# First stage in pieces as its loads land, and the output norms of two of three mixers moved out of the stage behind the third

## The chip, the cores and the metric

The kernel runs on one core of one Trainium2 chip. The metric is the time of one execution on the device in microseconds (us), the median of three runs. Smaller is better. Engines are called PE (TensorE: matmuls; PEld is its weight load), DVE (VectorE), ACT (ScalarE), POOL (GpSimd) and SP (SyncE, which here only starts DMAs).

## The reference

One inference step of a network of two layers over 640 tokens: 128 context tokens and 512 latent ones, model width 1024, float32. In a layer, `_ada` gives shift, scale and gate from a conditioning vector; the three mixers work on column groups of one projection; each ends in a group norm and a gate.

```python
def _rms_norm(x, g, eps=1e-6):
    xf = x.astype(jnp.float32)
    y = xf * lax.rsqrt(jnp.mean(xf * xf, axis=-1, keepdims=True) + eps)
    return (y * g.astype(jnp.float32)).astype(x.dtype)

def _group_norm(y, g, n_groups, center, eps=1e-5):
    yf = y.reshape(y.shape[:-1] + (n_groups, y.shape[-1] // n_groups))
    if center: yf = yf - jnp.mean(yf, axis=-1, keepdims=True)
    yf = yf * lax.rsqrt(jnp.mean(yf * yf, axis=-1, keepdims=True) + eps)
    return yf.reshape(y.shape) * g

mod = silu(cond) @ ada_w + ada_b                       # six vectors of 1024: sh1, sc1, g1, sh2, sc2, g2
h = _rms_norm(x, norm1_g) * (1 + sc1) + sh1
u = h @ w_in                                           # 1024 x 3296
# SSD (Mamba-2), 8 heads of 64, 512 columns, forward and backward scan over chunks of 128 tokens
y_ssd = _group_norm((y_f + y_b + d_skip * xs) * silu(z), ssd_norm_g, 2, center=False)
# RWKV-7, 4 heads of 64, 256 columns
y_rwkv = _group_norm(o_f + o_b, rwkv_norm_g, 4, center=True) * gate
# mLSTM, 4 heads of 64, 256 columns
y_ml = _group_norm(h_f + h_b, mlstm_norm_g, 4, center=True) * sigmoid(o)
x = x + g1 * (concat([y_ssd, y_rwkv, y_ml]) @ w_out)
h = _rms_norm(x, norm2_g) * (1 + sc2) + sh2
x = x + g2 * ((silu(h @ ffn_w1) * (h @ ffn_w3)) @ ffn_w2)
```

Outputs are the normed `x` of both token groups and the final states of the context scans of each layer and direction.

## The kernel before

All engines are programmed by hand. Each has one stream of instructions, and they wait on semaphores; nothing is reordered by a planner, so the order is the written one.

**Layout.** `x` stays in SBUF feature-major: 8 tiles (KT) of 128 features by 640 tokens. Tokens go in five chunks of 128 (NC), chunk 0 being the context. `U` holds the projected tiles: Z to Z+3 the SSD's gate, XS to XS+3 its values, later its output, MV and MV+1 mLSTM's output, BT_ and CT_ RWKV's, and LORA, MISC, MO the gates. `arena` is one area that is used again and again.

**Weights.** SP loads blocks of 128 columns (512 KB) in the order of the list BLOCKS into a ring of four slots (`ring`); ada_w's groups g (512 columns, four units each) have slots of their own. A product in full precision is three fp32r matmuls: ScalarE's `split` (line 1647) writes the high part of a weight block to `whi`, GpSimd (line 810) the low part in place, and TensorE does high·high, high·low, low·high (`mm3`, lines 928 to 930) over two halves of 320 tokens. The activations have high and low parts too (`rwp_r`, `arena_r`; for w_out `rp_r` and `U_r`).

**Stages of a layer,** times of the first in us:
- 0 to 57, in the first layer alone: loads, 40 transposes of `x` (line 826), squares (ScalarE, 1603), sums over features by VectorE (2001) and by ones products (`norm_sum`, 848 and 852), root (1608), reciprocal, the row spread to all partitions (`norm_rows`, 879), the product with `x` (1989); ada_w's groups 0, 2, 1, 3 (`ada_unit` 892, `ada_pick` 900, `ada_copy` 1634); ScalarE writes h (`norm_out`, 1622). GpSimd builds the constants first (553 to 642) and counts them in `setup["pool"]`, which others wait on up to POOL_SET.
- to about 290: the projections, 26 blocks in the order of ORDER. The first is the mixed block MISC (RWKV's last 64 columns, dt, mLSTM's gates), whose pieces SP loads as runs of 16 to 256 bytes, in six transfers.
- to 395: the scans of SSD and mLSTM chunk by chunk. TensorE makes scores, VectorE multiplies by weights (2273), then SSD's product of 16 (line 1183) and mLSTM's; `normalise` (2314 is its last instruction) divides mLSTM's output by its denominator, and four products by `ident` (1240) add both directions and turn the result to feature-major.
- to 580: RWKV in five rounds of 37 us, one for each chunk. In each, products of keys and masks (VectorE 2384 to 2395, 2412, 2425), an inversion by repeated products (TensorE 1317, VectorE's additions 2405), then the output, added to U (2458).
- 580 to 613: the norms of all three mixers' outputs. The mean of BT_/CT_ and MV/MV+1 by block sums (`g_job`, TensorE 1462, float32), the centring (VectorE 2475), squares, sums, root of 640 columns (ScalarE, 1892 on), reciprocal (2488), the spreading (1462), the scaling of eight tiles with gains (2505) and gates (2510), the low parts (2493). GpSimd's `gates` multiplies SSD's four tiles by Z beforehand.
- w_out (8 blocks; the third block's split comes only when a block before it is done), the second norm, the FFN (to about 1150).

The lines that say how the first stage begins:

```python
pe.wait_ge(setup["in"], 80)                  # all of x and three small loads
...
pe.wait_ge(setup["par"], 16 * DEPTH * (len(PROWS) + 2))   # parameters of both layers
...
norm_sum(0)
norm_rows(0)
pe.wait_ge(setup["pool"], POOL_SET)
pe.wait_ge(setup["dve"], 1)
for i, g in enumerate(EARLY):
    for u in range(UNITS):
        ada_unit(0, g, u)
```

Of the kernel before, what the change touches and what calls it, by code (L numbers as in the profile page):

```python
# [22 lines left out]
F32 = mybir.dt.float32  # L23
F32R = mybir.dt.float32r
BF16 = mybir.dt.bfloat16
ALU = mybir.AluOpType
# [3 lines left out]
P = 128  # L30
# [46 lines left out]
for _name, _rows in (("ada_b", 48), ("norm1_g", 8), ("norm2_g", 8), ("ssd_conv_w", 18), ("ssd_conv_b", 6),  # L77
# [18 lines left out]

POOL_IDENT, POOL_SET = DEPTH + 3, 87
# [3 lines left out]
    "g_mm": 14, "g_read": 6, "g_rec": 2, "g_sq": 8, "g_src": 1, "g_std": 2, "gated": 1, "inv_add": 50,  # L101
# [9 lines left out]
    "y_done": 8, "y_half": 4, "y_hi": 8, "y_lo": 8, "y_mm": 5, "ym_ready": 5, "yr_mm": 10, "yr_read": 10,  # L111
    "ys_read": 5, "yt_mm": 5, "yt_read": 5,
# [7 lines left out]
    "pair_mm", "pair_read", "tmp_act", "tmp_dve", "feat_ready", "k_scaled",  # L120
    "rows_act", "rows_dve", "kk_sq", "lora_x", "rw_ready",
# [6 lines left out]
    "g_src", "g_sq", "g_mm", "g_read", "g_std", "g_done", "wo_mm", "wo_read", "ffn_mm", "ffn_silu", "ffn_ready",  # L128
# [4 lines left out]
def build(nc, io):  # L133

    with ExitStack() as ctx:
        def sb(name, n):
# [6 lines left out]
                 ("pool", "in", "par", "cs", "mm", "read", "dve", "act")}  # L143
# [4 lines left out]
                  for l in range(DEPTH)]  # L148

# [22 lines left out]
        NSD, NRC = sb("NSD", NC), sb("NRC", NC)  # L172
        SELr = ctx.enter_context(nc.sbuf_tensor("SEL", [P, 6 * NC], F32R))
# [69 lines left out]
        YM = ar(8960, 512).rearrange("p (d n) -> p d n", d=2)  # L243

# [35 lines left out]
        SQUARES = [gtmp[:, 0, :], gtmp[:, 1, :], U[:, Z + 2, :], U[:, Z + 3, :]]  # L280
# [24 lines left out]
        EARLY = [0, 2, 1, 3]  # L305
        UNITS = KT // 2
# [9 lines left out]
        BLOCKS = [(0, "ada_w", g, u) for g in EARLY[:2] for u in range(UNITS)]  # L316
        BLOCKS += [(0, "w_in", m) for m in ORDER[:2]]
# [25 lines left out]
        for n, b in enumerate(BLOCKS):  # L343
# [15 lines left out]
            total[q] += 16 * (6 if b[1:] == ("w_in", MISC) else 1)  # L359
# [13 lines left out]
        at_block = {b: n for n, b in enumerate(BLOCKS)}  # L373
        SPLIT = [n for n, b in enumerate(BLOCKS) if b[1] != "ada_w"]
# [8 lines left out]
        POST = [m for m in ORDER if m in CONV or m in SHIFT]  # L383
        YTILES = [XS, XS + 1, XS + 2, XS + 3, BT_, CT_, MV, MV + 1]
        SHIFTED = {m: i for i, m in enumerate(SHIFT)}
# [8 lines left out]
        with nc.Block() as block:  # L394
            @block.sync
            def _(sp):
# [3 lines left out]
                def state(name, l):  # L400
# [3 lines left out]
                sp.dma_start(xi[:, 0, :], io["x_prompt"].rearrange("a t f -> (a t) f")).then_inc(setup["in"], 16)  # L404
                sp.dma_start(xi[:, 1:NC, :], io["x_sample"].rearrange("a (c p) f -> p (a c) f", p=P)).then_inc(
                    setup["in"], 16)
# [6 lines left out]
                for lay in range(DEPTH):  # L413
# [52 lines left out]

                    def rwkv_out():
# [23 lines left out]
                    for n in range(first_, end_):  # L491
                        blk = BLOCKS[n]
                        l, name = blk[0], blk[1]
                        if blk == (0, "w_in", ORDER[2]):
                            sp.wait_ge(setup["pool"], POOL_SET)
                            small_loads(0)
                        if blk == (lay, "w_in", ORDER[24]):
                            rows_out()
                        if blk == (lay, "w_out", 0):
                            rows_in()  # L500
                            states_in()
                            states_out()

                            sp.wait_ge(s["yt_read"], at["yt_read"] + NC)
                        if blk == (lay, "w_out", RING):
                            rwkv_out()
# [17 lines left out]
                        if blk[1:] == ("w_in", MISC):  # L524
                            gt = C_GATE
                            for at_, n_, src in ((0, 64, C_RW + 896), (64, 16, C_DT)):
                                load(dst[:, :, at_:at_ + n_], w[:, :, src:src + n_], sem)
                            for at_, src in ((80, gt + 4), (112, gt)):
                                load(dst[:, :, at_:at_ + 4], w[:, :, src:src + 4], sem)
                                load(dst[:, :, at_ + 4:at_ + 8], w[:, :, src + 8:src + 12], sem)  # L530
# [17 lines left out]
            def _(pool):  # L548
# [67 lines left out]

                for c, (lo, hi) in enumerate(((0, 8), (8, 16), (16, 20), (20, 24), (0, 16), (16, 24))):
# [28 lines left out]
                for lay in range(DEPTH):  # L646
# [26 lines left out]
                    def gates():  # L673

                        pool.wait_ge(s["yt_read"], at["yt_read"] + NC)
                        pool.wait_ge(s["ys_read"], at["ys_read"] + NC)
                        g.tensor_tensor(U[:, XS:XS + 4, :], U[:, XS:XS + 4, :], U[:, Z:Z + 4, :], ALU.mult).then_inc(
                            s["gated"], 1)
                        pool.wait_ge(s["gated"], at["gated"] + 1)
                        pool.wait_ge(s["rw_ready"], at["rw_ready"] + 1)  # L680
# [9 lines left out]
                    def end_values(c):  # L690
# [8 lines left out]
                        ins.then_inc(s["ve_ready"], 1)  # L699

# [16 lines left out]
                    def scans():  # L717
# [18 lines left out]
                        for c in range(2, NC):  # L736
                            scaled_values(c)
                            skip(c)

# [42 lines left out]

                    n = at_block[lay, "w_in", MISC]
                    if before[n] is not None:
                        sem, value = used[before[n]]
                        pool.wait_ge(sem, value)
                    w = slot(n)
                    g.memset(w[:, :, 88:112], 0.0)
                    g.memset(w[:, :, 120:128], 0.0).then_inc(s["gaps"], 1)
                    for q in range(Q_LAYER):  # L790
# [16 lines left out]
                        q_ = lay * Q_LAYER + q  # L807
# [1787 lines left out]
```

## Time and profile before

| | |
|---|---|
| three runs | 2306.55, 2297.8, 2301.24 us |
| median | 2301.24 us |
| the profiled execution | 2307.51 us, span 2305.8 us |
| mean granted clock of PE | 0.962 of full speed |
| PE busy | 2129.9 us (92%) |
| DVE busy | 836.0 us (36%) |
| ACT busy | 774.3 us (34%) |
| POOL busy | 735.9 us (32%) |

The span is the time between the first and the last record of the profile, and the execution takes a little more. A share is busy time over the whole span, so it says nothing of a single stage; for those, the rows below give stretches.

### The profile page before, as it was taken

Reading aid. Unit: us, or ns where it says so; the run is one execution under the profiler, and the core shown is the slowest. Engines: PE = TensorE matmul, PEld = TensorE weight load, DVE = VectorE, ACT = ScalarE, POOL = GpSimd, SP = SyncE. Lnnn points to the kernel's source line nnn. Section 1 sums busy time; section 2 is a strip of 40 time slices with the busy share of each in tenths; the row PEclk is TensorE's granted clock in tenths of the full one; section 3 lists DMA queues with packets and bytes.
Section 4 is the critical chain, followed back from the end, with each engine's and each line's share of the span. In section 5 each row is a group of like instructions: output and inputs, shape, how many; then the busy total and the mean of one; then the engine's idle time right before and its main releaser. Section 6 shows DMA issues by size and latency. Waiting matters only on the chain.

```text
span 2305.8 us, 46139 instructions
## 1 busy us (share of the span) xinstructions
PE 2129.9 (92%) x20590; PEld 1974.0 (86%) x20590; DVE 836.0 (36%) x1385; ACT 774.3 (34%) x1368; POOL 735.9 (32%) x539
## 2 busy tenths in 40 slices
PE   4999999888789999999979989988888899999999
PEld 4999766778589999999979987667867899999998
DVE  4755265554641111011148443555455311110112
ACT  3535553323333222121144364433332422222212
POOL 4333161324123333333313322522242233333331
PEclk7999998999899999999989999899998899999999
DMA  7454201000012222234335431010001122222222
GB/s 250 147 156 128 63 8 37 6 2 3 19 55 65 80 76 74 74 110 142 104 87 174 148 114 30 1 38 5 3 2 46 50 79 74 74 74 74 73 76 71
DMA packets 260497, 166.67 MB, mean 72 GB/s; under 512 B 29938, under 2 KB 234228, under 8 KB 260300
## 3 DMA queue, kind: packets, MB, share of 16 engines
q1 hardware_dynamic: 259846, 163.59, 23.9%
q8 instruction: 162, 2.65, 0.5%
q14 instruction: 35, 0.29, 0.1%
q10 hardware_dynamic: 454, 0.14, 0.0%
HBM read 159.59 MB, written 4.12 MB: 71 GB/s over the span
## 4 chain that ended last, share of the span: by engine, by line
PE 84%; DVE 7%; ACT 5%; issue 2%; POOL 1%; DMA 0%; another core or an unknown queue 0%; SPq 0%; DVEq 0%; ACTq 0%
PE PS L928 21%; PE PS L929 20%; PE PS L930 20%; PE PS L1317 5%; PE PS L892 2%; PE PS L1462 1%; PE PS L1146 1%; PE PS L1383 1%; PE PS L1335 1%; PE PS L1183 1%; PE PS L989 1%; DVE U L2330 1%; PE PS L1197 1%; POOL ring_r L810 1%; PE PS L1150 1%
## 5 line engine op out<-in xcount | busy, mean ns | idle before, releaser
L928 PE MATMUL PS<-rwp_r,whi_r 128*128 128x320 f32 x2880 | 904.5, 314 | 40.4 <-POOL ring_r L810 16.5
L930 PE MATMUL PS<-rwp_r,ring_r 128*128 128x320 f32 x2880 | 896.6, 311 | 0.0
L810 POOL TENSOR_TENSOR ring_r<-ring,whi_r 128x1024 fp32r<-128x1024 f32 (+1 forms) x204 | 498.5, 2445 | 1139.7 <-ACT whi_r L1647 1139.7
L929 PE MATMUL PS<-arena_r,whi_r 128*128 128x320 f32 x2240 | 697.4, 311 | 0.0
L928 PEld LDWEIGHTS PS<-rwp_r,whi_r 128*128 128x128 f32 x2880 | 547.0, 190 | 56.0 <-issue 28.6
L930 PEld LDWEIGHTS PS<-rwp_r,ring_r 128*128 128x128 f32 x2880 | 546.9, 190 | 0.0
L929 PEld LDWEIGHTS PS<-arena_r,whi_r 128*128 128x128 f32 x2240 | 425.4, 190 | 0.0
L1647 ACT ACTIVATE whi_r<-ring 128x1024 fp32r<-128x1024 f32 (+1 forms) x204 | 211.4, 1039 | 542.1 <-PE PS L930 542.0
L929 PE MATMUL PS<-U_r,whi_r 128*128 128x320 f32 x960 | 298.2, 311 | 0.0
L2542 DVE TENSOR_TENSOR U<-arena,PS 128x640 f32<-128x640 f32 x44 | 36.2, 822 | 549.7 <-PE PS L930 549.7
L929 PEld LDWEIGHTS PS<-U_r,whi_r 128*128 128x128 f32 x960 | 181.8, 189 | 0.0
L1317 PE MATMUL PS<-arena 64*64 64x64 f32 x3840 | 137.2, 223 | 37.3 <-DVE arena L2393 17.1
L1317 PEld LDWEIGHTS PS<-arena 64*64 64x64 f32 x3840 | 124.5, 138 | 50.0 <-DVE arena L2393 19.9
L2001 DVE TENSOR_TENSOR arena<-arena 128x640 f32<-128x640 f32 x30 | 63.1, 2104 | 213.4 <-ACT arena L1603 212.9
L1918 ACT ACTIVATE arena<-PS 128x640 f32<-128x640 f32 x44 | 31.0, 705 | 263.4 <-PE PS L930 263.4
L1676 ACT ACTIVATE U<-PS 128x640 f32<-128x640 f32 x56 | 39.3, 702 | 181.8 <-PE PS L930 181.5
L1849 ACT ACTIVATE arena<-PS 128x512 f32<-128x512 f32 (+1 forms) x100 | 55.5, 555 | 132.7 <-PE PS L1317 132.7
L1817 ACT ACTIVATE arena<-PS,arena 128x128 f32<-128x128 f32 x240 | 65.6, 390 | 77.2 <-PE PS L1150 77.0
L769 POOL TENSOR_TENSOR arena<-arena,MKC 128x256 f32<-128x256 f32 x40 | 36.6, 935 | 145.7 <-DVE arena L2388 145.7
L2521 DVE SCALAR_TENSOR_TENSOR x<-PS,MOD,x 128x128 f32<-128x128 f32 (+2 forms) x96 | 36.0, 431 | 125.2 <-PE PS L930 125.2
L2065 DVE SCALAR_TENSOR_TENSOR arena<-U,PC,arena 128x127 f32<-128x127 f32 x80 | 61.9, 794 | 24.8 <-ACT arena L1688 22.9
L2405 DVE TENSOR_TENSOR arena<-arena,PS 128x256 f32<-128x256 f32 x100 | 40.4, 419 | 69.8 <-PE PS L1317 69.8
(383 smaller groups left out, 2667.7 us busy)
## 6 DMA issues: line engine op xcount, KB each, us to landing
ring<-in_ffn_w SPq DMA_DIRECT2D x120, 512.0 KB, 3.8
rwp<-in_ada_w SPq DMA_DIRECT2D x64, 512.0 KB, 4.8
ring<-in_w_in SPq DMA_DIRECT2D x50, 512.0 KB, 4.4
U<-in_ada_w SPq DMA_DIRECT2D x16, 512.0 KB, 9.7
ring<-in_w_out SPq DMA_DIRECT2D x16, 512.0 KB, 4.6
arena<-in_ada_w SPq DMA_DIRECT2D x16, 512.0 KB, 4.7
ring<-in_ffn_w SPq DMA_DIRECT2D x16, 384.0 KB, 3.3
out<-arena SPq DMA_DIRECT2D x5, 512.0 KB, 2.6
```

The costliest lines, as they stand in the source:

```text
L810: g.tensor_tensor(rings_r[:, slot_of[n], 0:size(n), :], slot(n)[:, 0:size(n), :], whis[:, q_ % 2, 0:size(n), :].bitcast(F32), ALU.subtract ...
L892: ins = mm(PS[32 * q:32 * q + 32, 2, 0:P], cT[:, 2 * k:2 * k + 32], slot(n)[:, k - 2 * u, q * P:(q + 1) * P], start=k == 0, stop=k == KT - 1)
L928: mm(out, w[0][:, k, :], hi[:, cols], start=start, stop=False)
L929: mm(out, w[0][:, k, :], lo[:, cols], start=False, stop=False)
L930: return mm(out, w[1][:, k, :], hi[:, cols], start=False, stop=stop)
L1317: ins = mm(PS[t_, 4 * d + bank, col0 + 64 * hh:col0 + 64 * hh + 64], b[lhs][t_, hh, :], IDC[t_, :] if rhs is None else b[rhs][t_, hh, :], ...
L1647: A(whis[:, q % 2, 0:size(n), :], slot(n)[:, 0:size(n), :], ACT.Copy).then_inc(s["split_hi"], 1)
L1817: ins = A(W[:, i, q * P:(q + 1) * P], PS[:, ROW_BANK[(9 * c + i) % 3], q * P:(q + 1) * P], ACT.Exp, bias=COLS[:, c, 1, r + q:r + q + 1])
L1849: A(b["QQ"][:, w], PS[:, a + 2, :].rearrange("p (w h t) -> p w h t", w=2, h=4)[:, w], ACT.Copy).then_inc(s["inv_copy"], 1)
L2001: v.tensor_tensor(rs, rs, tmp[:, k % 2, :], ALU.add).then_inc(s["sq_used"], 1)
L2065: return v.scalar_tensor_tensor(out=out, in0=in_, scalar=s, in1=out, op0=ALU.mult, op1=ALU.add)
L2405: v.tensor_tensor(b["X"], b["X"], heads(PS[:, 4 * d + 3, 0:256], 4), ALU.add).then_inc(s["inv_add"], 1)
```

## The change

**First stage.** `x` is loaded in five transfers, one per chunk, on semaphores x0, x2 and x4, and the transposes wait for a pair of chunks each. The mixed block's columns come in three transfers (64, 16 and 16 columns); GpSimd's `gaps` then puts the gates' columns where they belong and clears the rest. The three transfers are spread: one ahead of all of ada_w, one ahead of group 2, one ahead of the second w_in block. ada_w's groups 0 and 2 and their picks go ahead of `norm_sum(0)` on TensorE. ScalarE copies them between its squares, loads the root's table early on a dummy, and splits the first two weight blocks between the norm's root and its row copy. VectorE makes the low parts of h between the products. GpSimd does `gaps` and the first two low parts ahead of several constants (POOL_CONST counts those before, POOL_SET all), and the wait for POOL_SET stands behind the first two blocks. The parameters of the second layer are no longer loaded at the start: SP issues them ahead of w_in's sixth block, and TensorE turns them at the fourth.

**Norms of SSD and mLSTM.** SSD: GpSimd gates each chunk as it comes (`gate(c)`), ScalarE squares it (`y_squares`). mLSTM: `normalise` adds both directions, subtracts the mean of each head, squares and sums token-major, in five more VectorE instructions, and two transposes replace four products. In RWKV's round 0, TensorE sums SSD's squares with 20 products into one column each; VectorE copies them; ScalarE takes the root of all 30 columns (YN) at the round's end; VectorE the reciprocal in round 1; TensorE turns them in round 2; SP writes the rows to DRAM and loads them back in three transfers, spread over all partitions. VectorE scales SSD's and mLSTM's tiles in rounds 2 and 3 and applies mLSTM's gate in round 4, where the high parts (ScalarE) and low parts (VectorE) of these six tiles are written.

**Behind RWKV** only RWKV's two tiles are normed, with root and reciprocal over 320 columns, and w_out's rows follow in the order YSEQ, put between the steps of that norm.

The core of the diff:

```diff
+        FIRST = [(0, "w_in", MISC), (0, "ada_w", EARLY[1], 0), (0, "w_in", ORDER[1])]
-        BLOCKS = [(0, "ada_w", g, u) for g in EARLY[:2] for u in range(UNITS)]
-        BLOCKS += [(0, "w_in", m) for m in ORDER[:2]]
+        BLOCKS = [(0, "w_in", ORDER[0])]
+        BLOCKS += [(0, "ada_w", g, u) for g in EARLY[:2] for u in range(UNITS)]
+        BLOCKS += [(0, "w_in", ORDER[1])]
+        YSEQ = [0, 1, 2, 3, 6, 7, 4, 5]
...
@@ SP, ahead of w_out's block 2 @@
+                    def norm_rows():
+                        sp.wait_ge(s["yn_read"], at["yn_read"] + 2)
+                        load(yn_d[lay].rearrange("r (c t) -> (r c) t", c=NC), YNT, s["yn_in"])
+                        sp.wait_ge(s["yn_in"], at["yn_in"] + 16)
+                        load(RBS, yn_d[lay][0:2].unsqueeze(0).broadcast_to((P, 2, T)), s["yn_in"])
+                        for q in range(2):
+                            load(ring_rows(lay)[64 * q:64 * q + 64],
+                                 yn_d[lay][2 + q:6:2].unsqueeze(0).broadcast_to((64, 2, T)), s["yn_in"])
+                        sp.wait_ge(s["y_done"], at["y_done"] + 6)
...
-                pe.wait_ge(setup["in"], 80)
+                    pe.wait_ge(setup["x%d" % (c - c % 2)], 16 * min(2, NC - (c - c % 2)))
...
                 pe.wait_ge(setup["read"], 2 * NC)
+                pe.wait_ge(setup["pool"], POOL_CONST)
+                pe.wait_ge(setup["dve"], 1)
+                for u in range(UNITS):
+                    ada_unit(0, EARLY[0], u)
+                params_turned(0, 6)
+                ada_pick(0, EARLY[0])
+                for u in range(UNITS):
+                    ada_unit(0, EARLY[1], u)
+                ada_pick(0, EARLY[1])
                 norm_sum(0)
                 norm_rows(0)
-                pe.wait_ge(setup["pool"], POOL_SET)
-                pe.wait_ge(setup["dve"], 1)
-                for i, g in enumerate(EARLY):
+                for i, g in enumerate(EARLY[2:]):
...
@@ PE, RWKV's rounds @@
+                        if k == 0:
+                            pe.wait_ge(s["rw_tok"], at["rw_tok"] + 2)
+                            pe.wait_ge(s["ysq_ready"], at["ysq_ready"] + NC)
+                            for c in range(NC):
+                                for q in range(4):
+                                    n = NC * (q // 2) + c
+                                    ins = mm(PS[:, 0, n:n + 1], U[:, Z + q, ck(c)], ones[:, 0:1], start=q % 2 == 0,
+                                             stop=q % 2 == 1)
+                            ins.then_inc(s["yn_mm"], 1)
...
@@ PE, behind RWKV @@
+                    for f in range(2):
+                        g_job(2 * f, [(BO[:, :], U[:, Z + f, :])]).then_inc(s["g_mm"], 1)
                     w01 = [split_block(Q_WOUT + m) for m in range(2)]
+                    out_rows(range(3))
+                    pe.wait_ge(s["g_src"], at["g_src"] + 1)
+                    for f in range(2):
+                        g_job(2 * f, [(BO[:, :], U[:, BT_ + f, :])]).then_inc(s["g_mm"], 1)
+                    out_rows(range(3, 4))
...
+                    out_rows(range(4, 6))
...
+                    out_rows(range(6, 8))
...
@@ ACT, the end of RWKV's round 0 @@
+                            act.wait_ge(s["yn_read"], at["yn_read"] + 1)
+                            A(YN[:, 0:2 * NC], YN[:, 0:2 * NC], ACT.Sqrt, bias=eps[:, 2:3], scale=1.0 / 256)
+                            A(YN[:, 2 * NC:], YN[:, 2 * NC:], ACT.Sqrt, bias=eps[:, 2:3], scale=1.0 / 64).then_inc(
+                                s["yn_std"], 1)
...
@@ DVE, normalise @@
+                        v.tensor_tensor(YS, YM[:, 0], YM[:, 1], ALU.add).then_inc(s["dve_step"], 1)
+                        v.tensor_reduce(YMEAN, heads(YS, 4), AX.X, ALU.add).then_inc(s["dve_step"], 1)
+                        v.scalar_tensor_tensor(out=heads(YM[:, 0], 4), in0=wide(YMEAN, 64), scalar=-1.0 / 64,
+                                               in1=heads(YS, 4), op0=ALU.mult, op1=ALU.add).then_inc(s["ym_ready"], 1)
+                        v.tensor_tensor(YM[:, 1], YM[:, 0], YM[:, 0], ALU.mult).then_inc(s["dve_step"], 1)
+                        v.tensor_reduce(YN[:, 2 * NC + c::NC], heads(YM[:, 1], 4), AX.X, ALU.add).then_inc(
+                            s["dve_step"], 1)
...
@@ DVE, RWKV's rounds @@
+                        if k == 2:
+                            dve.wait_ge(s["yn_mm"], at["yn_mm"] + 2)
+                            v.tensor_copy(YNT, PS[0:6 * NC, 0, 0:P]).then_inc(s["yn_read"], 1)
+                            if l == 0 and k == 2:
+                                dve.wait_ge(s["yn_in"], at["yn_in"] + 16 * 4)
+                                ssd_scaled(range(2))
```

## Rows read from the trace of the kernel before

**Rows 1.** The page's first line.

```profile
span 2305.8 us, 46139 instructions
```

**Rows 2.** Busy time by stretch: us, PE PEld DVE ACT POOL, PEclk, DMA share, GB/s.

```profile
0.00:57.00 57.00, 25.66 (x338) 23.27 (x338) 23.41 (x36) 20.18 (x35) 28.53 (x95) 0.79 0.79 253
16.00:20.00 4.00, 3.17 (x26) 2.61 (x24) 3.93 (x9) 0.80 (x5) 3.13 (x14) 1.00 1.06 385
21.00:26.00 5.00, 0.00 (x0) 0.00 (x0) 4.34 (x6) 3.90 (x7) 4.06 (x10) 0.67 0.80 69
354.00:366.00 12.00, 11.93 (x54) 8.32 (x55) 4.94 (x11) 3.46 (x13) 1.81 (x2) 0.50 0.00 1
580.00:613.00 33.00, 20.94 (x81) 11.38 (x82) 24.17 (x22) 12.60 (x18) 4.14 (x2) 0.80 0.00 1
```

**Rows 3.** The chain of waits behind RWKV, first layer: start us, us, what.

```profile
580.05 4.59 PE PS L1462 x16
...
592.99 1.28 ACT L1892
...
627.92 1.07 ACT whi_r L1647
```

**Rows 4.** Groups by line, 580 to 613 us: busy, mean ns, idle before.

```profile
L2488 DVE RECIPROCAL arena<-arena 64x640 f32<-64x640 f32 (+1 forms) x2 | 8.2, 4115 | 2.9 <-ACT arena L1892 2.9
...
L2505 DVE SCALAR_TENSOR_TENSOR U<-U,PC,PS 128x640 f32<-128x640 f32 x6 | 4.9, 854 | 0.0
```

**Rows 5.** GpSimd's timeline at the end of RWKV: start, duration, instruction, idle before.

```profile
579.46 4.69 POOL L810 TENSOR_TENSOR ring_r<-ring,whi_r 128x1024 fp32r<-128x1024 f32 x2 [10.40 <-ACT whi_r L1647]
```

**Rows 6.** The chain of waits, 0 to 160 us.

```profile
2.51 8.80 DMA arena<-in_final_norm_g
11.35 6.76 PE PS L826 x40
...
26.75 2.27 PE PS L848 x10
...
52.07 0.27 ACT arena L1634
...
57.40 0.25 PE PS L928
...
71.34 1.06 ACT whi_r L1647
```

**Rows 7.** ScalarE's timeline in the first stage, two of eight tiles.

```profile
46.49 1.19 ACT L1622 ACTIVATE arena<-arena,MOD,GS 128x128 f32<-128x128 f32 x2
...
48.35 1.19 ACT L1622 ACTIVATE arena<-arena,MOD,GS 128x128 f32<-128x128 f32 x2
```

**Rows 8.** VectorE's timeline behind normalise, between two chunks of the scans.

```profile
380.44 1.28 DVE L2273 TENSOR_TENSOR arena<-arena,PS 128x512 f32<-128x512 f32 x2 [0.20 <-PE PS L1117]
```

**Rows 9.** TensorE's timeline: at that boundary, in RWKV's round 0, and a norm's sums.

```profile
381.36 1.05 PE L1240 MATMUL PS<-ident,arena 128*128 128x128 f32 x8
...
382.34 1.09 PE L1183 MATMUL PS<-arena 128*64 128x128 f32 x16
...
404.09 1.15 PE L1317 MATMUL PS<-arena 64*64 64x64 f32 x32 [0.87 <-DVE arena L2393]
...
675.96 1.27 PE L852 MATMUL PS<-ones,arena 128*128 128x1 f32 x10 [0.99 <-ACT arena L1603]
```

**Rows 10.** VectorE's timeline in RWKV's rounds 2 and 4.

```profile
477.56 0.95 DVE L2395 TENSOR_TENSOR arena<-arena,MKC 128x256 f32<-128x256 f32 x1
...
494.25 0.42 DVE L2405 TENSOR_TENSOR arena<-arena,PS 128x256 f32<-128x256 f32 x1 [3.87 <-PE PS L1317]
...
559.28 0.42 DVE L2405 TENSOR_TENSOR arena<-arena,PS 128x256 f32<-128x256 f32 x1 [0.51 <-PE PS L1317]
...
561.54 1.35 DVE L2425 TENSOR_TENSOR arena<-PS,PP 128x512 f32<-128x512 f32 x2 [0.91 <-ACT arena L1858]
```

**Rows 11.** ScalarE's timeline at the start of RWKV's round 1.

```profile
441.04 0.60 ACT L1849 ACTIVATE arena<-PS 128x512 f32<-128x512 f32 x1 [2.14 <-PE PS L1317]
```

More of the change, by code:

```diff
@@ L95 @@
 RING = 4
+POOL_CONST = DEPTH + 10
 POOL_IDENT, POOL_SET = DEPTH + 3, 87
@@ L142, in build @@
         setup = {n: ctx.enter_context(nc.semaphore("s_" + n)) for n in
-                 ("pool", "in", "par", "cs", "mm", "read", "dve", "act")}
+                 ("pool", "in", "par", "cs", "mm", "read", "dve", "act") + tuple("x%d" % c for c in range(0, NC, 2))}
         tail = {n: ctx.enter_context(nc.semaphore("t_" + n)) for n in
@@ L148, in build @@
                   for l in range(DEPTH)]
+        yn_d = [nc.dram_tensor("yn%d" % l, (6, NC * P), F32, kind="Internal").ap() for l in range(DEPTH)]
         PS = ctx.enter_context(nc.psum_tensor("PS", [P, 8, 512], F32))
@@ L524, in _ @@
                         if blk[1:] == ("w_in", MISC):
[L525 to L530, printed above, removed]
+                            for dst, a in mixed_parts(l):
+                                load(dst, a, sem)
                         elif name == "ffn_w2":
@@ L738, in scans @@
                             skip(c)
+                            gate(c - 2)
+                        for c in range(NC - 2, NC):
+                            gate(c)
                     def chunk_keys(k):
@@ L780, in rwkv @@
                         gates()
[L783 to L790, printed above, removed]
+                    if lay:
+                        gaps(lay)
+                    for q in range(0 if lay else 2, Q_LAYER):
                         if q == 8 and lay == 0:
@@ new lines, in _ @@
+                    ins.then_inc(s["g_mm"], 1)
+                    out_rows(range(4, 6))
+                    pe.wait_ge(s["g_rec"], at["g_rec"] + 1)
+                    for f in range(2):
+                        for hf in range(2):
+                            rows = slice(64 * hf + 32 * f, 64 * hf + 32 * f + 32)
+                            ins = mm(PS[:, 2 * f + hf, 0:HALF], SPREAD[rows, :], gtmp[rows, 3, 0:HALF], start=True,
+                                     stop=True)
+                        ins.then_inc(s["g_mm"], 1)
@@ L1835, in _ @@
                     decays(0)
+                    for c in range(NC - 2, NC):
+                        y_squares(c)
                     for k in range(NC):
@@ L2418, in _ @@
                             prep_scan(k + 1)
+                        else:
+                            for f in range(2):
+                                v.tensor_tensor(U[:, MV + f, :], U[:, MV + f, :], U[:, MO + f, :],
+                                                ALU.mult).then_inc(s["y_done"], 1)
+                            for n in range(2):
+                                y_low(n)
+                        if k == 1:
+                            dve.wait_ge(s["yn_std"], at["yn_std"] + 1)
+                            v.reciprocal(YN[:, :], YN[:, :]).then_inc(s["yn_rec"], 1)
                         adds(1, 2)
@@ L2517, in residual @@
+                    for n in range(6, 8):
+                        y_low(n)
                     def residual(b, m, row, sem):
```

365 lines of the change are left out of this document (209 added, 156 removed).

## The prediction

> **What bounds the kernel now.** I read the page first, then the chain of waits, then busy time by stretches, then the timelines of single engines where a term needed them. The profiled execution spans 2305.8 us and took 2307.5 us; the median of the three runs is 2301.2, so I work out a difference on the trace and take it from 2301.2 [rows 1]. TensorE sets the end nearly everywhere: the chain of waits runs through matmuls, and only two stretches that the change touches are different. In the first 57 us TensorE works 25.7 us. In the 33 us behind RWKV it works 20.9 us at a mean clock of 0.80, while VectorE works 24.2 us [rows 2]. The chain names the reason there: ones and block sums, a load of ScalarE's table, a reciprocal over 640 columns at 4.1 us, then the scaling of eight tiles, one behind the other; only then does w_out start [rows 3, 4].
>
> The end of one such stage I take at the split of w_out's third block, since that waits for the first: from T0 (the last addition into RWKV's output, first block sum at 580.05) to 627.92 it is 47.9 us [rows 3]. Layer 1 shows the same length.
>
> **The stage behind RWKV, per layer.** What stays behind T0 is RWKV's own norm; SSD's four and mLSTM's two tiles come normalised, and their rows of w_out fill TensorE's waits. Steps by rows:
> - A float32 matmul over 320 columns is two passes of 4.59 / 16 = 0.287 us [rows 3]; the two tiles' block sums (8 passes) take 2.3 us. An fp32r matmul of a w_out row takes 13.94 us / 96 = 0.145 us [rows 6], so one of the eight steps over k, 12 matmuls for two blocks, takes 1.75 us.
> - w_out's splits stay behind ScalarE's last RWKV copy: GpSimd ends them at 579.46 + 4.69, T0 + 4.1 [rows 5]. So three steps run from T0 + 4.1 to 9.4, RWKV's second sums to 11.7, a step to 13.4. The sums' wait for VectorE (two products of 0.82, an addition of 1.5) is over by T0 + 5, inside those steps.
> - Centring and squaring follow the sums tile by tile and end at 13.4; 8 passes of squares to 15.7; two steps to 19.2. Beside them ScalarE takes a root of 320 columns and VectorE a reciprocal of 320, half of 4.1 us: ready at 18.5 [rows 4].
> - Spreading, 8 passes, to 21.5. VectorE scales at 0.85 a tile, multiplies by the gate, and writes two low parts, ending at about 25.4 [rows 4]. The last two steps end at 28.2. TensorE has idled 3.1 us by then, and I add 0.7 for a clock that may be half for part of the rest.
>
> 28.9 in place of 47.9: 19.0 us less, 38.0 for both. Bounds are 15 (clock at half for all that follows the idling) and 21 (the splits come earlier, nothing idles).
>
> **The first stage.** Today everything starts at the last of five small and large loads, landed at 2.51 + 8.80 = 11.3 us; 40 transposes end at 18.1; the norm's sums start at 26.8; ScalarE writes h at 1.86 us a tile and picks up ada_w's third group only behind four of them, at 52.07; the projections start at 57.4, and the first two blocks end at 71.3 [rows 6, 7]. Loads move 385 GB/s, but only 69 GB/s in 21 to 26 us, when the mixed w_in block comes in runs of 16 to 256 bytes [rows 2].
> With x in chunks, chunks 0 and 1 (1.05 MB) land at about 7.3 (2.5, 2 for the first bytes, 2.7 at 385 GB/s), all of it at 11.3, so 16, 16 and 8 transposes of 0.169 end at 14.6 instead of 18.1. The queue then brings ada_w's groups 0 and 2 with two parts of the mixed block: 4.5 MB at 385 GB/s and two runs of small pieces, landed at about 24.0: 9.1 for x and what small loads lie among it, 11.7 for the 4.5 MB, 1.0 and 2.2 for the two runs of pieces, which I take from what is left of the slow 5 us. TensorE's units and the pick end at 25.1, the sums (20 passes, as 2.27 per ten at the low clock) at 29.5, root, reciprocal and row copy at 33.3; four units of group 1 let ScalarE start at 35.4. Three tiles of 1.86 and group 3's copy bring the projections' start to 41.6. GpSimd's constants (it is busy for 28.5 of the 57 us [rows 2], less than half of it with these) move behind the first two splits, under the projections. Then TensorE is the bound: 14.0 us, and 2 us for a clock still low: 57.7. That is 13.6 us less than 71.3. Bounds: 8 (each of three hand-overs 2 us late) and 17 (clock high at once). Layer 1's parameter loads, small ones on the sync queue ahead of a w_in block, cost nothing: that block is wanted some 18 us later.
>
> **SSD and mLSTM stage, per layer.** TensorE is the bound. normalise gets five dependent VectorE instructions over 256 columns, three of them ahead of what TensorE waits for. One such instruction is 0.42, about 0.45 to 0.5 with its wait [rows 10]. VectorE goes on to SSD's weights 0.2 us behind it, two of them take 1.28, and TensorE starts SSD's matmuls 2.1 us behind that end of normalise (380.24), at 382.34 [rows 8, 9]. With 2.4 us more in front, the first of those two ends at 2.4 + 0.2 + 0.64, and TensorE, as now 0.6 us behind a weight's end, starts at 3.8: 1.7 us late, in three of the four chunk boundaries 5.1. In the fourth, at half clock, TensorE was itself late and gains 1.2 from two transposes in place of four products (8 passes now take 1.05 at full clock [rows 9]). At the end of the last chunk 1.2 more stands on the path. GpSimd's gate per chunk (an estimate from 4.69 us for 2048 columns [rows 5]: 1.2 us for 512) can hold VectorE's scan there, 0.7. Sum +5.8; bounds +2 (reductions overlap) and +12 (one more stretch at half clock as long as 354 to 366, worth 6 us [rows 2]).
> ScalarE's squares (half a microsecond a chunk) lie in its waits, and cost nothing; without that cover, 0.6 us a chunk, inside the upper bound.
>
> **RWKV, per layer.** In chunk 0, 20 one-column products, 40 passes at 1.27 / 10 = 0.127 or less, say 4.5 us, stand ahead of the inversion [rows 9]. TensorE waited 0.87 us at 404.09, and I take as much for the second direction; both are swallowed, and +2.8 is left. Chunk 1's reciprocal of 30 columns is 30 / 640 of 4.1: +0.2. In chunk 4, two gates and two low parts (3.1 us) stand ahead of an addition. VectorE waits there 0.51 us, as much before the next, and 0.91 before the product behind them, 1.9 in all, so at least 1.2 is late; as each addition feeds the next matmul it may be all 3.1: I take +2.0 [rows 10]. The other instructions of 640 columns stand in waits like the 3.87 us ahead of 494.25 and cost nothing [rows 10]. Sum +5.0; bounds +2 and +8 (each of ten covers short by 0.3).
> The rows go out to memory and back (15 KB, then 1.31 MB) between chunk 2's masks, that end at 478.5, and the addition that ends at 495.5 [rows 10]: 2.2 + 2.2 + 3.4 us at 385 GB/s is 8 of 17 us, so no stall. The sync queue stands at this wait and at the one for the last gates; behind it are w_out's blocks 2 and 3 only, wanted at 627.9 and later.
> ScalarE's root at the end of chunk 0 needs another table: 1.28 us [rows 3]. Then come chunk 1's copies, two of which wait 2.14 us for TensorE at 441.04 [rows 11], so it costs nothing; its other copies of 640 columns go into waits of that kind too. The Trainium skill (ScalarE: Activation LUTs, What ACT_TABLE_LOAD costs) counts a drain on top, 2.66 us for a switch; by the row the switch is over in 1.3, and by the page half a microsecond a layer would be added.
>
> **The sum.** -13.6 - 38.0 + 11.6 + 10.0 = -30.0 us; 2301.2 - 30.0 = 2271. Everything else, FFN above all, is unchanged.
>
> **Rivals.**
> 1. *The moved work is not hidden.* Both added terms at their upper bounds: -13.6 - 38 + 24 + 16 = -11.6, 2290. For it: TensorE fell to half clock for 354 to 366 although it was busy 11.93 of 12.00 us [rows 2], so a stage with more waits may fall again. Against it: that it fell once in a layer, at the same place. The skill's rule (TensorE: Matmul & The Clock Gate, HAM oscillation) ties a fall to idling between bursts of matmuls; the row does not agree for this stretch, and by the rule alone waits of 1.7 us would cost themselves only. Chance 0.18.
> 2. *The first stage gives 5 us only*, because groups 0 and 2 of ada_w, now ahead of the norm's sums, come late or GpSimd's splits hold VectorE's products: 2280. Chance 0.12.
> 3. *w_out's six early steps find no low parts*, because the y instructions of chunk 4 run late, so they follow RWKV's chain as before: 25.4 + 14 = 39.4 us in place of 47.9, -8.5 a layer; -13.6 - 17 + 21.6 = -9.0, 2292. Against it: VectorE's room in chunk 4. Chance 0.06.
> 4. *Slower:* the three broadcast loads come back late and VectorE stands in chunk 2. At 385 GB/s they take 3.4 us; at the 69 GB/s of 21 to 26 us, 19 us, ending at about 502, 7 us late; at a third of that, which the smallest runs there may have reached (an estimate), 57 us, 45 late in each layer: +90 - 30, 2361. It decides from a landing 32 us after the masks (15 us late in each layer cancels 30). Against it: runs are 2.5 KB. Chance 0.04.
> 5. *More than forecast*, with bounds on the good side in two or three terms: 2254. Chance 0.10.
>
> The forecast itself has 0.50, with a range of its own of 2262 to 2280. The range 2254 to 2290 adds cases 2, 5 and half of 1. A difference under 0.5% (11.5 us) is about what these runs cannot tell from none, so faster means below 2289.7: 0.5 + 0.12 + 0.10, half of 1 and a third of 3 make 0.83; within 0.5% the rest of these, 0.13; slower 0.04.
>
> **What the profile after would show.** First two blocks of the projections over near 58 us; T0 to the third split of w_out near 29 us; between the SSD stage's chunks TensorE waiting for VectorE's weights, 1 to 2 us each; one run of 40 short passes in chunk 0; no wait of VectorE for a load in chunk 2. Wrong if the clock's low stretches in the two middle stages grow, or if the first stage's projections start later than 46.

## The result: 1.2% slower where 1.3% faster was forecast

The changed kernel takes 2326.2 us (median of 4 runs, 2323.8 to 2329.9) against 2299.6 before: ratio 1.0122, interval 1.0093 to 1.0151. Forecast were 2271, range 2254 to 2290. It is the case "slower by over 0.5%", to which I gave 0.04, and not by the mechanism that I named for it. One execution of the experiments, of sums_early, took 2650 us at a mean granted clock of 0.73, and no number below has it.

The page's first lines, then busy time by stretches (columns as in [rows 2]): both layers' scans, RWKV of the first layer, what follows it.

```profile
span 2328.2 us, 46071 instructions
...
PE 2154.9 (93%) x20508; PEld 1999.9 (86%) x20516; DVE 852.7 (37%) x1435; ACT 774.3 (33%) x1375; POOL 746.5 (32%) x551
...
308.00:406.00 98.00, 83.87 (x643) 55.38 (x651) 58.24 (x114) 36.56 (x127) 37.78 (x47) 0.85 0.04 12
1454.00:1555.00 101.00, 88.43 (x662) 58.44 (x670) 59.99 (x115) 36.84 (x128) 38.80 (x47) 0.80 0.04 11
406.00:594.00 188.00, 164.25 (x3529) 148.98 (x3519) 101.38 (x243) 63.34 (x142) 51.80 (x57) 0.94 0.06 16
...
594.00:625.00 31.00, 23.89 (x128) 20.64 (x128) 15.94 (x17) 6.62 (x9) 5.21 (x2) 0.89 0.00 1
```

The same two stages of the kernel before:

```profile
319.00:403.00 84.00, 80.65 (x704) 55.87 (x705) 47.43 (x89) 33.74 (x121) 32.63 (x41) 0.91 0.09 24
...
403.00:580.00 177.00, 153.18 (x3460) 138.50 (x3452) 89.72 (x228) 56.97 (x132) 56.09 (x58) 0.97 0.02 4
```

The scans grew from 84 to 98 and 101 us and the clock there fell from 0.91 to 0.85 and 0.80; RWKV grew from 177 to 188 and its clock fell from 0.97 to 0.94. TensorE has fewer instructions than before and is busy 25 us longer.

I cut both profiles at the same events (the third weight block's split; SSD's first product; the first mask of each RWKV round; T0; w_out's third split). Differences of after to before in us, first and second layer:

| stretch | forecast | measured |
|---|---|---|
| first stage | -13.6 | -12.6 |
| stage behind RWKV | -19.0, -19.0 | -18.2, -18.4 |
| scans of SSD and mLSTM, up to RWKV's first mask | +5.8, +5.8 | +14.2, +16.8 |
| RWKV's round 0 | +2.8, +2.8 | +7.3, +7.1 |
| rounds 1 to 3 | +0.2, +0.2 | +0.5, +4.0 |
| round 4 | +2.0, +2.0 | +3.2, +3.4 |
| all the rest | 0 | +15.1 |

The columns sum to -30 and to +22.4, by which the two spans differ. Both gains came as forecast. What was wrong is the price of the moved work, 25.5 in place of 10.0 in RWKV and 31.0 in place of 11.6 in the scans, and 15.1 us that no term held.

The first stage after, by the chain of waits, and the stage behind RWKV by the same view:

```profile
15.30 8.38 DMA U<-in_ada_w
23.72 3.34 PE PS L968 x64
...
58.72 1.06 ACT whi_r L1749
```

```profile
592.83 1.07 ACT whi_r L1749
593.97 5.25 POOL ring_r L694 x2
599.31 0.38 PE PS L1010
...
606.36 2.15 PE PS L1567 x8
...
624.18 1.07 ACT whi_r L1749
```

58.72 answers to 71.34 in [rows 6]. T0 is now 594.5: w_out starts at T0 + 4.8 (forecast 4.1), RWKV's second sums end at T0 + 14.0 (11.7), the third split stands at T0 + 29.7 (28.9), where [rows 3] has 47.9.

### The profile page after: what moved, and what is told of

Same layout as the page of the kernel before. It is cut to its first block, busy times and chain, and to the rows that moved or that the text cites. A ratio compares the mean times of both kernels' runs of the same rounds, so it can differ in the third digit from the quotient of the medians.

```text
span 2328.2 us, 46071 instructions
## 1 busy us (share of the span) xinstructions
PE 2154.9 (93%) x20508; PEld 1999.9 (86%) x20516; DVE 852.7 (37%) x1435; ACT 774.3 (33%) x1375; POOL 746.5 (32%) x551
## 4 chain that ended last, share of the span: by engine, by line
PE 84%; DVE 6%; ACT 5%; issue 2%; POOL 1%; SPq 1%; DMA 0%; another core or an unknown queue 0%; DVEq 0%; ACTq 0%; POOLq 0%
PE PS L1010 21%; PE PS L1012 20%; PE PS L1011 20%; PE PS L1418 5%; PE PS L968 2%; PE PS L1270 1%; POOL ring_r L694 1%; PE PS L1440 1%; PE PS L1284 1%; PE PS L1076 1%; PE PS L1488 1%; DVE U L2455 1%; PE PS L1233 1%; ACT arena L1921 1%; ACT whi_r L1749 1%
## 5 line engine op out<-in xcount | busy, mean ns | idle before, releaser
L1418 PE MATMUL PS<-arena 64*64 64x64 f32 x3840 | 144.5, 230 | 37.8 <-DVE arena L2551 20.0
L1418 PEld LDWEIGHTS PS<-arena 64*64 64x64 f32 x3840 | 131.6, 144 | 50.2 <-issue 19.8
```

What stands on the lines that cost most here:

```text
L1418: ins = mm(PS[t_, 4 * d + bank, col0 + 64 * hh:col0 + 64 * hh + 64], b[lhs][t_, hh, :], IDC[t_, :] if rhs is None else b[rhs][t_, hh, :], ...
```

## What a boundary between two chunks looks like after the change

VectorE's timeline behind normalise, then TensorE's at the same place, between chunks 2 and 3:

```profile
358.29 0.69 DVE L2426 TENSOR_TENSOR arena<-PS,arena 128x512 f32<-128x512 f32 x1
359.01 0.42 DVE L2430 TENSOR_TENSOR arena<-arena 128x256 f32<-128x256 f32 x1
...
360.85 0.42 DVE L2439 TENSOR_REDUCE YN<-arena 128x4 f32<-128x256 f32 x1
361.30 2.48 DVE L2385 TENSOR_TENSOR arena<-arena,PS 128x512 f32<-128x512 f32 x4
```

```profile
360.40 0.44 PE L1326 MATMUL PS<-ident,arena 128*128 128x128 f32 x2
362.64 1.09 PE L1270 MATMUL PS<-arena,whi 128*64 128x128 f32 x16 [1.80 <-DVE arena L2385]
363.67 1.29 PE L1284 MATMUL PS<-U,arena 64*64 64x128 f32 x16
```

The five instructions take 2.3 us (2.4 in the forecast), and TensorE waits 1.8 us for the weights. SSD's first 16 products still take 1.09 us, as in [rows 9]; the 16 behind them, 1.09 at full clock, take 1.29 here, and 1.97 at other boundaries: the clock has gone to half behind the wait. A chunk takes 19.7 us (342.93 to 362.64) where one at full clock took 15.0 (331.14 to 346.15, before): 1.6 of the 4.7 are the wait and 3.1 work at half clock. That split can be read, since in one layer of a later run (lows_late, the scans as here) the same waits stand and the clock stayed: chunks of 16.6 and 16.7 us. The same boundary there:

```profile
359.05 1.09 PE L1270 MATMUL PS<-arena,whi 128*64 128x128 f32 x16 [1.79 <-DVE arena L2385]
360.07 1.09 PE L1284 MATMUL PS<-U,arena 64*64 64x128 f32 x16
```

The 3.1 us are those of the two usual chunks. The half clock behind a boundary is not always that long: the chunk that begins at 362.64 took 18.1 us, and one in the second layer, at half clock for nearly all of it, 24.6 (1468.70 to 1493.34).

RWKV's round 0 shows the second place: the 20 one-column products, then the first levels of the inversion and RWKV's products.

```profile
406.55 6.67 PE L1405 MATMUL PS<-ones,U 128*128 128x1 f32 x40
413.14 3.68 PE L1418 MATMUL PS<-arena 64*64 64x64 f32 x64
416.75 3.11 PE L1440 MATMUL PS<-arena 64*128 64x256 f32 x16
```

At full clock the 64 passes take 2.08 us and the 16 products 2.00 (the run sums_wide, below). The burst is 6.7 us, not 4.5, and the half clock behind it costs 2.7 us more.

## Experiments

Theory A, the clock: TensorE's new waits, and the burst of one-column products, let the clock fall, and the work behind them costs more than the waits. Theory B, delay: the added instructions themselves are the cost, where and whenever they run.

Medians in us; each ratio is to the kernel before in the same batch, with its interval. "Chunk" is the middle one of three times in layer 0, each from one chunk's first SSD product to the next one's. The last two columns are of one profile each. A difference of two medians from different batches carries that of the batches too: the kernel before had 2299.6, 2300.1, 2300.1 and 2296.8 in them.

| run | median | ratio | chunk | scans, both layers, to before | round 0 |
|---|---|---|---|---|---|
| changed kernel | 2326.2 | 1.0122 (1.0093 to 1.0151) | 19.7 | +14.2, +16.8 | +7.3, +7.1 |
| first_only | 2291.5 | 0.9957 (0.9935 to 0.9980) | 15.0 | -5.9, -5.2 | -1.5, 0.0 |
| warm_scans | 2292.9 | 0.9973 (0.9950 to 0.9996) | 16.6 | +4.7, +9.4 | +4.1, +5.7 |
| sum_only | 2270.0 | 0.9886 (0.9829 to 0.9944) | 15.2 | -0.2, -3.2 | +5.6, +7.2 |
| sums_early | 2323.4 | 1.0104 (1.0070 to 1.0138) | 19.7 | +23.1, +26.3 | -1.5, +1.4 |
| reorder | 2288.5 | 0.9954 (0.9925 to 0.9984) | 14.9 | -3.4, +3.9 | +2.6, +5.7 |
| reorder_warm | 2284.3 | 0.9933 (0.9896 to 0.9969) | 15.1 | -2.6, +1.6 | +2.6, +5.6 |
| sums_wide | 2317.4 | 1.0087 (1.0049 to 1.0125) | 19.7 | +20.0, +11.9 | +1.1, +2.6 |
| lows_late | 2319.7 | 1.0085 (1.0056 to 1.0114) | 16.6 | +6.7, +18.6 | +5.7, +4.1 |
| two_late | 2297.3 | 1.0005 (0.9981 to 1.0029) | 15.6 | +0.8, -0.2 | +4.1, +4.1 |
| combined | 2273.6 | 0.9902 (0.9864 to 0.9940) | 14.8 | +1.9, -2.7 | +2.6, +2.6 |
| combined_pool | 2264.3 | 0.9859 (0.9827 to 0.9890) | 15.3 | -3.1, -3.3 | +1.1, +2.6 |

The kernel before itself ran between 2286 and 2309 us in one batch of 17, at mean clocks of 0.972 to 0.963 (up to 2319 us at 0.957 in another): its low stretches come and go too, so a difference of one profile below some 6 us in a stage is no evidence, and the readings below are those that repeat from chunk to chunk, or the medians.

### The first stage alone

The hunks of the first stage on the kernel before, nothing of the norms.

> The kernel before with the first stage's part of the change alone. By the traces the first stage gave 12.6 us (the split of the third weight block at 58.72 in place of 71.34), and nothing of it should be given back: 2287 us. Rival: the gain is lost later, because a part of the 22 us that the changed kernel is slower comes from this part (its loads of layer 1's parameters, the later wait for GpSimd's constants): 2295 or more.

8.6 us faster by the medians. The interval, 4.6 to 15 us, holds the forecast, and its edge touches the rival. The profile decides between them: its first stage is 10.4 us shorter, and no stretch behind it is longer than before by more than 2 us. So this half of the change is a gain, and all of the loss is in the other.

### Filling TensorE's wait

```diff
                             mlstm_back(c - 1)
+                            warm(6, 7)     # six products of 512 bf16 columns into bank 7, not used
                         y_ssd(c, 0)
```

> The changed kernel with six filler matmuls of 512 bf16 columns into an idle PSUM bank, where TensorE waits 1.8 to 2.2 us for VectorE's weights at each of the four chunk boundaries of the scans. Clock theory: of the 4.7 us that each boundary grew by, 1.6 is the wait and 3.1 is work at half clock behind it; with the wait filled the clock stays and 8 x 3.1 = 25 us come back less at most 4 for fillers that overrun: 2301 to 2308 us, and the products of SSD and its states behind the wait at 1.09 us again in place of 1.97. Delay theory (the later weights are all of it, the clock's stretches are as many as before): no change, or slower by the fillers: 2326 to 2330.

33 us less than the changed kernel, with every added instruction in place and 48 more on TensorE. The same boundary:

```profile
354.03 1.46 PE L1076 MATMUL PS<-NEG,identb 128*128 128x512 bf16 x6
355.99 1.09 PE L1270 MATMUL PS<-arena,whi 128*64 128x128 f32 x16 [0.50 <-DVE arena L2386]
357.01 1.09 PE L1284 MATMUL PS<-U,arena 64*64 64x128 f32 x16
```

TensorE starts SSD's products no earlier behind its transposes than it did, 2.2 us; only it wasn't idle. The products right behind are at full clock at all eight boundaries, and a chunk takes 16.6 us, as in the layer that kept its clock; one in layer 1 takes 21.9, with a low stretch inside it. Delay forecast 2326 or more; it is out as the main cause. The size of the gain is another matter. Of the 37 us between the two profiles 17 lie in the scans, where I had expected at least 21, 5 in round 0, and 15 in stretches that the fillers don't touch (9 of them in RWKV's rounds 1 to 3), whose low stretches come and go.

### Leaving mLSTM's norm out of normalise

One addition in place of the five instructions.

> The changed kernel whose normalise only adds both directions of mLSTM (one VectorE instruction of 256 columns in place of five); mean, centring, squares and their sum are left out, so mLSTM's norm is wrong by that. Clock theory: the wait falls below what sets the clock back, and the scans return to the length before, 14.5 and 16.2 us less, less 8 x 0.46 for the one that stays: 2326 - 27 = 2299 us. Delay theory: only the 8 x 1.8 us of the four instructions are gained: 2312.

2270, 56 us less than the changed kernel and 29 below what the clock theory gave. Four instructions of 0.46 us at ten places are 18 us, so some twice as much is clock. It shows what is at stake and not more, since the two theories both wanted a gain.

### The same instructions in another order

```diff
                         for i in range(4):
+                            if i == 2 and c:
+                                norm_tail(c - 1)      # the five instructions of normalise
                             weights(c, i)
...
-                        if c:
-                            mlstm_back(c - 1)
                         y_ssd(c, 0)
+                        if c:
+                            mlstm_back(c - 1)
```

> The changed kernel in another order: VectorE makes the next chunk's first two weights right behind normalise's fourth instruction and the five added ones behind them; TensorE turns mLSTM's output behind the first half of SSD's products. The five instructions stay, only the wait they cause is gone. Clock theory: the wait at a boundary falls from 2.2 to under 1 us and the half clock behind it with it; scans near the length before plus 3 us: 2326 - 22 = 2304 us. Delay theory (VectorE's added work costs wherever it stands): the weights 2 and 3 come 2.3 us late instead, TensorE waits there: 2320 or more.

> The kernel of the run reorder with three filler matmuls ahead of SSD's first products of each chunk. If a wait of 1 us still sets the clock back there, this is 6 to 10 us faster than reorder, 2296; if not, it is the same or up to 3 us slower.

reorder gains 38 us on the changed kernel with all of its work done (22 in the forecast); by the profiles 30 of them lie in the scans. VectorE's timeline and TensorE's at a boundary of it:

```profile
348.31 1.29 DVE L2385 TENSOR_TENSOR arena<-arena,PS 128x512 f32<-128x512 f32 x2 [0.25 <-PE PS L1204]
349.52 0.42 DVE L2433 TENSOR_TENSOR arena<-arena 128x256 f32<-128x256 f32 x1
```

```profile
349.66 1.09 PE L1270 MATMUL PS<-arena,whi 128*64 128x128 f32 x16 [0.32 <-DVE arena L2385]
350.68 1.09 PE L1284 MATMUL PS<-U,arena 64*64 64x128 f32 x16
```

The wait is 0.32 us, and the chunks of layer 0 take 14.8 to 15.4 us: the five instructions cost at most 0.4 a chunk here. Layer 1 has one chunk of 19.9, a low stretch such as the kernel before has in each layer, and the waits at the boundaries ahead of it are 0.3 to 0.6 us. Fillers on top (reorder_warm) gave 4 us in the medians, within both intervals: a wait of 0.3 us needs none.

### Half of it: two of the five behind the weights

```diff
+                    def norm_tail(c):      # called between weights(c + 1, 1) and weights(c + 1, 2)
                         v.tensor_tensor(YM[:, 1], YM[:, 0], YM[:, 0], ALU.mult)
                         v.tensor_reduce(YN[:, 2 * NC + c::NC], heads(YM[:, 1], 4), AX.X, ALU.add)
```

> The changed kernel with only the last two of the five added instructions of normalise (square and sum, 0.9 us) behind the next chunk's first two weights; TensorE's order as changed. TensorE's wait at a boundary is then 1.3 us, between the 0.3 to 0.5 of reorder, behind which the clock stayed full at all boundaries, and the 1.8 to 2.2 of the changed kernel, behind which it fell at all. By delay alone 8 x 0.9 = 7 us are gained, 2319; if the clock stays full behind 1.3 us, 25 more, 2294 to 2300; between these if it falls at some.

I had put the wait at 1.3 us; it is 0.76:

```profile
358.24 1.09 PE L1270 MATMUL PS<-arena,whi 128*64 128x128 f32 x16 [0.76 <-DVE arena L2385]
359.26 1.09 PE L1284 MATMUL PS<-U,arena 64*64 64x128 f32 x16
```

Moving 0.9 us at a boundary, 7 us in all, gained 29 us, and by the profiles the scans gave 30. The median, 2297, is what I had forecast for a clock that stays full, though with a shorter wait than I had put there. The clock was full behind all eight boundaries. With the waits of 1.8 to 2.2 us, which stand at 27 boundaries in the four profiles that have the changed kernel's scans (its own, sums_early, sums_wide, lows_late), it fell or was low behind 24; the three others are lows_late's first. What a wait between 0.76 and 1.8 us does here no run shows.

### RWKV's round 0: the burst of one-column products

```diff
-    ins = mm(PS[:, 0, n:n + 1], U[:, Z + q, ck(c)], ones[:, 0:1], ...)
+    n = 48 * n
+    ins = mm(PS[:, 0, n:n + 48], U[:, Z + q, ck(c)], ones[:, 0:48], ...)
```

> The changed kernel whose 20 one-column products in RWKV's round 0 multiply by 48 equal columns of ones in place of one (the sums are the same, each is there 48 times). Theory: the burst counts as idle for the clock since a pass streams one column; with 48 it counts as work, the 3.1 us for 16 passes and 3.7 for 64 behind it are 2.0 and 1.8 again, 2 x 3 us gained, less 40 x 0.02 us for the columns: 2322. Rival: the clock behind the burst is low for another reason (the wait ahead of it): 2327 to 2330.

```profile
414.40 4.67 PE L1405 MATMUL PS<-ones,U 128*128 128x48 f32 x40
419.00 2.08 PE L1418 MATMUL PS<-arena 64*64 64x64 f32 x64
421.01 2.00 PE L1440 MATMUL PS<-arena 64*128 64x256 f32 x16
```

48 times the columns take 2 us less, since they stay at full clock: 4.67 in place of 6.67, and 2.08 and 2.00 behind in place of 3.68 and 3.11. Round 0 is at +1.1 and +2.6. The medians gave 9 us, with overlapping intervals, so the round's own rows decide, and they repeat: behind the one-column burst the 64 passes take 3.1 to 3.7 us in all 14 layers of the seven profiles that have it in round 0, and behind the 48 columns 2.08 in five of six layers (3.17 in combined's first).

> The changed kernel with the 20 one-column products ahead of RWKV's round 0, where TensorE ran eight fillers while it waited some 6 us for GpSimd's keys. Both their own 6.7 us (1.7 of it lay in waits before) and the half clock behind them (2.4 us) go from round 0: 2 x 7.3 = 14.6 us, 2312 us, and round 0 at 35.8 us again. Rival: the wait for the keys is shorter than the burst, or the clock is low behind it just the same: 4 to 8 us gained only, 2318 to 2322.

That one, sums_early, moved the burst ahead of round 0, in place of eight fillers, and gave nothing that the noise would show: 2323 us for 2312. Round 0 came down by 8.9 us and the time ahead of it grew by 8.9 (layer 1: 5.7 and 9.5; a part of that growth is low stretches inside the scans).

```profile
408.16 6.46 PE L1370 MATMUL PS<-ones,U 128*128 128x1 f32 x40 [0.75 <-DVE U L2385]
414.49 1.09 PE L1381 MATMUL PS<-ident,arena 128*128 128x128 f32 x4
```

GpSimd's first keys were there at 410.98, so only 2.8 us were free, not 6, and the transposes behind the burst take 1.09 in place of the 0.60 that they take in the changed kernel, where fillers stand ahead of them. The burst took its half clock along.

### Round 4

```diff
-                            for n in range(2):
-                                y_low(n)       # between RWKV's first additions
+                            if k == 4 and n == 0:
+                                y_low(3)       # before the wait for the right sides; y_low(4) behind it
```

> The changed kernel whose two low parts of round 4 (1.5 us) move from between RWKV's first additions to the later waits of that round (1.50 and 1.95 us in the trace). If those 3.1 us at that place cost what round 4 grew by (3.2 and 3.4 us), 1.5 us a layer come back, 2323 us, within noise: read from round 4's length, not from the median. Rival: the two gates alone make the delay, and round 4 stays at +3.2.

Round 4 stands at +1.0 and 0.0, and at +0.7 and 0.0 in combined, which has the same edit. In the eight profiles that keep the two low parts where they were, it is +3.2 to +3.4 in 12 layers and +1.9 in four. In the changed kernel the four instructions take 4.3 us, where I had 3.1:

```profile
569.94 2.23 DVE L2567 TENSOR_TENSOR U<-U 128x640 f32<-128x640 f32 x2
572.10 2.07 DVE L2508 TENSOR_TENSOR U_r<-U,rwp_r 128x640 fp32r<-128x640 f32 x2
```

They take 0.82 us each at other places and 1.0 to 1.1 here. GpSimd is at work beside them (two instructions, 567.87 to 575.92), but that it is the cause no run isolates. In lows_late the medians moved by 6.5 us, more than the 5.6 of the two rounds, with the three spared boundaries in it, so only the length of round 4 counts as its result.

### All together

> The changed kernel with three edits of earlier runs together: normalise's five instructions behind the next weights (reorder), the sums over 48 equal columns (sums_wide), the two low parts of round 4 later (lows_late). The parts are in different stretches, so they should add: reorder's 2288 less 12 for the sums and 4 for the low parts: 2272 us, 1.2% faster than the kernel before. Rival: the clock's low stretches only move elsewhere, and it stays at reorder's 2285 to 2290.

> The kernel of the run combined with mLSTM's two gates on GpSimd behind round 3's keys, in place of VectorE between round 4's first additions. If these 1.6 us are what is left of round 4's growth, it is back at 31.0 us in each layer: 1 to 2 us less, 2270. Rival: GpSimd's two instructions, at some 1.6 us each, hold up the masks that it makes at the start of round 4, and it is 1 us slower.

combined came out at 2273.6 us for 2272 forecast, so the parts add as far as the noise lets one see. Its profiled execution was a long one (2286 us), with one chunk of 19.7 us in layer 0. combined_pool takes mLSTM's two gates from VectorE to GpSimd, behind round 3's keys. It has the lowest median, 1.4% below the kernel before and 62 us below the changed one. Round 4 is at 0.0 in both layers, 0.7 us less than combined's in the first; the other 8 us between the two medians are not shown to come from the gates, and the intervals overlap. Busy time in its scans, same columns:

```profile
308.00:389.00 81.00, 71.52 (x644) 47.85 (x651) 60.16 (x114) 36.83 (x128) 40.05 (x48) 0.98 0.05 14
```

VectorE is busier than in the changed kernel (60.2 against 58.2 us) and TensorE's clock is 0.98 in place of 0.85.

## Why the prediction was wrong

- **First stage**, right: -12.6 for -13.6. **Stage behind RWKV**, right: -18.2 and -18.4 for -19.0, with each of its steps within 2.3 us; in first_only the first stage alone gave 10.4. The broadcast rows (rival 4) were back in time: VectorE had no wait for a load in chunk 2, and the second of the three landed some 6 us behind its issue; the 15 KB on the way out took 3.1 us, not 2.2.
- **Scans, the step that failed.** "it starts at 3.8: 1.7 us late" was right (3.7 behind the same instruction, and 1.6 us a chunk where the clock stayed). What failed is that this was the whole price of a boundary. The clock was at half behind the wait at seven of eight boundaries, for 3.1 us of added time in the usual chunk; the eighth has no wait, since TensorE came to it late and still at half clock. Rival 1 had the right sign, "a stage with more waits may fall again", and I gave it 0.18 and, in the upper bound, one more low stretch a layer, where there were three or four. Against it I held that the clock "fell once in a layer" before and that by a rule "waits of 1.7 us would cost themselves only". The half clock at 354 to 366 in [rows 2], at a TensorE that was busy 11.93 of 12.00 us, shows that it can fall without a wait, and nothing of what waits do.
- **The rule I leaned on.** The Trainium skill (TensorE: Matmul & The Clock Gate, HAM oscillation, and the section behind it on a second failure mode) says that idling between groups of matmuls makes the clock go down and up, in the second case already by idles that are short and frequent. The trace agrees with the second: of the boundaries with a wait of 1.8 to 2.2 us 24 of 27 have half clock behind them, and two_late's eight with 0.76 none. The first, which I had used alone, is about longer gaps than these, and here the measurement decides.
- **RWKV, round 0:** the term "say 4.5 us" is what the passes take at full clock (4.6 in reorder); here it was 6.7, and the 2.7 us that half clock cost behind it had no term: +7.3 and +7.1 for +2.8. **Round 4:** +3.2 and +3.4 for +2.0; the four instructions take 4.3 us, not 3.1, and some 3.3 of them are late, which is the upper of the two ends.
- **The root's table** cost nothing, as forecast: from round 0's last transposes to round 1's first mask it is 3.62 us in both kernels. The load took 1.28 us at 447.00 and the next activation began at 448.29, with nothing on top, as I had read from the row.
- **The rest, +15.1**, is settled in part. 1.3 us in each layer stand behind w_out's third split: TensorE waits there 2.7 us for low parts in both kernels, but restarts at half clock in the changed one (0.47 us a matmul) and at full clock before (0.31). Another 2.6 and 1.1 us stand at the second norm. The other 9 us have no cause that a run shows; this sum was 3 us in combined_pool's profile. Why single stretches fall without a wait ahead of them, in the kernel before too, stays open.
- **The chances.** I added the moved work as sums of delays and left the clock, a cause common to them, to rival 1, so all terms were low together, and "Both added terms at their upper bounds" (2290) was no outer limit.

## What to carry to other kernels

Where TensorE is the bound and its clock can fall, price a new wait of it by the work that comes behind at half clock too, and not by its own length alone; moving 0.9 us of VectorE's work past TensorE's next operand gained 29 us here. Put added work on a helper engine behind what TensorE waits for next, and if a wait of that length must stay, fill it with idle products (behind reorder's 0.3 us they gave nothing that the noise would show). A burst of one-column products had the same half clock behind it as a wait, and with 48 equal columns the burst took no longer.

## What was not expected of the hardware

- 40 float32 passes of one column took 6.67 us; 40 of 48 columns took 4.67. In the run reorder the one-column burst began at full clock and took 4.63 us, and the half clock came behind it all the same (3.10 and 2.54 us for what takes 2.08 and 2.00).
- The same program ran between 2286 and 2309 us, at mean clocks from 0.972 to 0.963. In sum_only, three runs gave 2264 to 2272 us at 0.968 to 0.969 and one, the profiled, 2295 at 0.955: here 1% of time goes with about 1% of clock.
- Fillers made the program faster: 48 more matmuls, 33 us less by the medians, of which the profiles show 17 in the scans.
